# A hybrid attention block in two layers on one core: the MLP's and the latents' norms by fp32r products with ones, one inverse for both latents, two turned products and a joined maximum moved

## The reference

```python
for l in range(DEPTH):
    xn = rms_norm(x, attn_norm[l])
    (nsa_q, kv_c, kv_s, kv_w, nsa_g, cq, ckv, k_rope_raw, gate_a, gate_b) = split_cols(xn @ w_in[l])
    o_a = nsa_attention(nsa_q, kv_c, kv_s, kv_w, nsa_g, cmp_pe[l], cmp_w1[l], cmp_w2[l], pos)
    o_b = mla_attention(cq, ckv, k_rope_raw, mla_q_norm[l], mla_kv_norm[l], mla_w_uq[l], mla_w_ukv[l], pos)
    x = x + (sigmoid(gate_a) * (o_a @ nsa_w_o[l]) + sigmoid(gate_b) * (o_b @ mla_w_o[l])) @ w_out[l]
    hn = rms_norm(x, mlp_norm[l])
    x = x + square(relu(hn @ w_up[l])) @ w_down[l]
return rms_norm(x, final_norm)

# in mla_attention: cq (256 wide) and ckv (128 wide) are the latents
q  = rms_norm(cq,  q_norm)  @ w_uq
kv = rms_norm(ckv, kv_norm) @ w_ukv
# rms_norm(x, g) = x * rsqrt(mean(x * x) + 1e-6) * g, over the last axis
```

## Time and profile before

| what | value |
|---|---|
| median of three runs | 1512.05 us (1511.93 to 1512.61) |
| the profiled execution | 1511.41 us |
| its span, first to last instruction | 1509.6 us |
| PE busy | 1487.3 us, 99% |
| DVE / ACT / POOL busy | 889.5 / 719.0 / 437.2 us |
| chain that ended last | PE 85%, ACT 5%, DVE 4%, issue 4% |

### The profile page before, as it was taken

How to read it: one execution, slowest core, us unless ns; L and a number is a source line. 1 busy time by engine, 2 the same in 40 slices (tenths; PEclk the granted TensorE clock), 3 DMA queues, 4 the chain that set the end, 5 groups by cost and what they waited for, 6 DMA issues and landing times.

```text
span 1509.6 us, 21031 instructions
## 1 busy us (share of the span) xinstructions
PE 1487.3 (99%) x7284; PEld 1245.0 (82%) x7284; DVE 889.5 (59%) x1543; ACT 719.0 (48%) x1312; POOL 437.2 (29%) x459
## 2 busy tenths in 40 slices
PE   8999999999999999999999999999999999999998
PEld 6888788887888888888888888888888888888886
DVE  6876766767553544535558776667575535354453
ACT  6864777873431222222367557888543222122222
POOL 1402677873020101101022046778711101010111
PEclk9999999999999999999999999999999999999999
DMA  6333121135323333333323521212432333332233
GB/s 212 125 129 134 67 85 64 57 99 181 92 90 98 98 97 97 97 97 98 98 85 125 175 84 64 78 50 82 133 121 85 97 98 98 97 97 97 97 97 112
DMA packets 43363, 154.29 MB, mean 102 GB/s; under 512 B 5441, under 2 KB 5441, under 8 KB 43281
## 3 DMA queue, kind: packets, MB, share of 16 engines
q1 hardware_dynamic: 37296, 133.77, 28.0%
q0 software_dynamic: 5696, 18.94, 3.5%
q10 hardware_dynamic: 288, 0.52, 0.1%
HBM read 142.73 MB, written 10.49 MB: 101 GB/s over the span
## 4 chain that ended last, share of the span: by engine, by line
PE 85%; ACT 5%; DVE 4%; issue 4%; DMA 1%; POOL 0%; POOLq 0%; DVEq 0%; SPq 0%; ACTq 0%
PE G L1530 14%; PE G L1531 13%; PE G L1532 13%; PE O L1532 9%; PE O L1531 9%; PE O L1530 9%; PE O L1822 3%; PE T L1799 3%; PE T L1530 2%; PE T L1532 2%; PE T L1531 2%; PE S L1774 2%; PE O L1605 1%; ACT wsplit L645 1%; PE S L1780 1%
## 5 line engine op out<-in xcount | busy, mean ns | idle before, releaser
L645 ACT ACTIVATE wsplit<-stage 128x1024 fp32r<-128x1024 f32 x227 | 240.1, 1058 | 593.1 <-PE G L1532 270.5
L1019 DVE TENSOR_TENSOR wsplit<-stage,wsplit 128x1024 fp32r<-128x1024 f32 x180 | 259.7, 1443 | 78.3 <-ACT wsplit L645 78.1
L631 POOL TENSOR_TENSOR F<-Y 128x512 f32<-128x512 f32 x64 | 68.4, 1069 | 637.3 <-DVE Y L1488 637.3
L1530 PE MATMUL G<-xg,wsplit 128*128 128x512 f32 x560 | 223.1, 398 | 7.9 <-DVE wsplit L1045 6.9
L1531 PE MATMUL G<-xg,wsplit 128*128 128x512 f32 x560 | 219.5, 392 | 0.0
L1532 PE MATMUL G<-xg,wsplit 128*128 128x512 f32 x560 | 219.4, 392 | 0.0
L529 POOL TENSOR_TENSOR wsplit<-stage,wsplit 128x1024 fp32r<-128x1024 f32 x46 | 111.2, 2418 | 124.8 <-ACT wsplit L645 124.3
L1258 DVE CUSTOM_DVE_ANT_0 F<-S,F 128x512 f32<-128x512 f32 (+3 forms) x176 | 89.1, 506 | 88.8 <-PE S L1774 60.9
L818 ACT ACTIVATE F<-F,nmx 128x512 f32<-128x512 f32 (+3 forms) x176 | 101.4, 576 | 65.2 <-DVE nmx L1258 62.8
L1530 PEld LDWEIGHTS G<-xg,wsplit 128*128 128x128 f32 x560 | 105.6, 189 | 29.7 <-DVE wsplit L1045 6.9
L1530 PE MATMUL G<-area,wsplit 128*128 128x512 f32 x320 | 124.7, 390 | 0.3
(11 more groups left out here) (300 smaller groups left out, 3042.0 us busy)
## 6 DMA issues: line engine op xcount, KB each, us to landing
stage<-units SPq DMA_DIRECT2D x229, 512.0 KB, 3.5
stage_n<-units_n SPq DMA_DIRECT2D x20, 512.0 KB, 3.7
gates<-Y POOLq DMA_DIRECT2D x32, 256.0 KB, 2.9
E<-gates POOLq DMA_DIRECT2D x24, 256.0 KB, 3.0
F<-gates POOLq DMA_DIRECT2D x8, 256.0 KB, 3.9
x<-x_in SPq DMA_DIRECT2D x3, 512.0 KB, 6.5
rope<-tables POOLq DMA_DIRECT2D x1, 768.0 KB, 6.7
out<-F SPq DMA_DIRECT2D x3, 256.0 KB, 2.3
```

The lines of the kernel that those rows point to most:

```text
L631: pool.tensor_tensor(F[:, m % 2, :], Y[:, m % 2, :], Y[:, m % 2, :], ALU.mult)\
L645: act.activation(wslot(u)[:, 0, :], staged(u), ACT.Copy).then_inc(s_whin if u in SN else s_whi, 1)
L1019: dve.tensor_tensor(wslot(u)[:, 1, :], staged(u), wslot(u)[:, 0, :], ALU.subtract)\
L1530: pe.matmul(dst, a(0), b(0), start=first, stop=False)
```

## The change

For the latents, ACT rounds the two sums of squares (`c_squares_hi`), POOL takes their rests, and behind `MISC` four fp32r products with a matrix of halves, zeros and ones leave the mean of `ckv`'s squares on half of the partitions and that of `cq`'s on the other half, in one bank. ACT takes one root of 128x512 (`c_root`), DVE inverts 128x512 at once (`c_inverse`, behind `W1 5`, that is behind the second gate), ACT copies the halves to the partitions that lack them (`c_factors`, behind `W2K`), and the three scalings (`c_norm`) go behind `W1 6`, behind `W1 7` and into step 1. For the MLP, ACT rounds the sum of squares, DVE takes the rest, PE adds over the partitions by two fp32r products in the second tile (`wide_sum`), ACT takes a root and DVE an inverse of 128x512; the split of `up`'s fourth unit goes ahead of the first square. `WT 0` and `WT 1` are in steps 10 and 12. The joined maximum stands behind `probs_lo`.

```diff
-FILL[11].append((("WT", 0), 0))
-FILL[13].append((("WT", 1), 0))
+FILL[10].append((("WT", 0), 0))
+FILL[12].append((("WT", 1), 0))
...
+            for n, value in enumerate((0.5, 0.0, 1.0)):
+                pool.memset(halves[:, 64 * n:64 * n + 64].bitcast(F32), value).then_inc(s_halves, 1)
...
+                pool.wait_ge(s_csqhi, l + 1)
+                pool.tensor_tensor(CSQ[:, 0:4:2, :], csq[:, 0:3:2, :], CSQ[:, 1:4:2, :], ALU.subtract).then_inc(s_csqlo, 1)
...
+            def squares_hi(l):
+                act.wait_ge(s_sqadd, l * (2 * KT) + 2 * KT)
+                act.activation(SQ[:, 0, :], F[:, 2, :], ACT.Copy).then_inc(s_sqhi, 1)
+            def wide_root(l):
+                act.wait_ge(s_sqall, l + 1)
+                act.activation(rs[:, :], SB[0][:, :], ACT.Sqrt, scale=1.0 / D, bias=eps).then_inc(s_wide, 1)
...
+                def c_squares_hi():
+                    act.wait_ge(s_csq, l * 3 + 3)
+                    act.wait_ge(s_csum, l + 1)
+                    act.activation(CSQ[:, 1:4:2, :], csq[:, 0:3:2, :], ACT.Copy).then_inc(s_csqhi, 1)
                 def c_root():
-                    act.wait_ge(s_cms, l + 1)
-                    for kind in range(2):
-                        ins = act.activation(crc[:, 1, kind, :], g_tile(("CM", 0))[:, QT * kind:QT * kind + QT], ACT.Sqrt,
...
+                    act.wait_ge(s_cspread, l + 1)
+                    act.activation(csq[:, 0, :], g_tile(("CB", 0))[:, :], ACT.Sqrt, scale=1.0 / 128, bias=eps)\
+                        .then_inc(s_croot, 1)
+                def c_factors():
+                    act.wait_ge(s_cinv, l + 1)
+                    act.activation(csq[0:64, 2, :], csq[64:128, 0, :], ACT.Copy)
+                    act.activation(csq[64:128, 2, :], csq[64:128, 0, :], ACT.Copy).then_inc(s_cfactor, 1)
+                    act.wait_ge(s_cfactor, l * 2 + 1)
+                    act.activation(csq[64:128, 0, :], csq[0:64, 0, :], ACT.Copy).then_inc(s_cfactor, 1)
...
                     if item == ("Q", 2):
-                        c_root()
+                        c_squares_hi()
                     if name == "MISC":
                         q_hi(2)
                         swap_key()
+                        c_root()
...
+                    if item == ("W2K", 0):
+                        c_factors()
...
                         if isinstance(f, int) and m == 0:
-                            root(l * 2 + 1)
-                        split_hi(l, U_MLP + m + 2, f)
+                            squares_hi(l)
+                        if not (isinstance(f, int) and m == 1):
+                            split_hi(l, U_MLP + m + 2, f)
                         if isinstance(f, int) and m == 0:
-                            spread(l * 2 + 1)
+                            wide_root(l)
+                            split_hi(l, U_MLP + m + 3, f)
...
+            def squares_lo(l):
+                dve.wait_ge(s_sqhi, l + 1)
+                dve.tensor_tensor(SQ[:, 1, :], F[:, 2, :], SQ[:, 0, :], ALU.subtract).then_inc(s_sqlo, 1)
+            def wide_factors(l):
+                dve.wait_ge(s_wide, l + 1)
+                dve.reciprocal(rs[:, :], rs[:, :]).then_inc(s_rsmlp, 1)
...
-                def c_diagonals():
...
+                def c_inverse():
+                    dve.wait_ge(s_croot, l + 1)
+                    dve.reciprocal(csq[:, 0, :], csq[:, 0, :]).then_inc(s_cinv, 1)
                 def c_norm(c):
-                    dve.wait_ge(s_cspread, l * 2 + (c // 2 + 1))
+                    dve.wait_ge(s_cfactor, l * 2 + 2)
                     gain = par[:, PR_QN + c:PR_QN + c + 1]
-                    dve.scalar_tensor_tensor(E[:, c, :], E[:, c, :], gain, g_tile(("CB", c // 2))[:, :],
+                    dve.scalar_tensor_tensor(E[:, c, :], E[:, c, :], gain, csq[:, c // 2 * 2, :],
...
                     if item == ("Q", 2):
-                        c_diagonals()
+                        dve.sem_inc(s_gfree, 1)
                     if name == "MISC":
                         q_lo(2)
                         key_sum()
-                        for c in range(3):
-                            c_norm(c)
+                        dve.wait_ge(s_croot, l + 1)
+                        dve.sem_inc(s_gfree, 2)
...
+                    if item == ("W1", 5):
+                        c_inverse()
+                    if item == ("W1", 6):
+                        c_norm(0)
+                    if item == ("W1", 7):
+                        c_norm(1)
...
                         max_of(i)
-                        if joins(i) is not None:
-                            max_of(joins(i))
...
                     if 0 <= i - LAG_SPLIT < NJ:
                         probs_lo(i - LAG_SPLIT)
+                    if joins(i) is not None:
+                        max_of(joins(i))
...
+                    if i == 1:
+                        c_norm(2)
...
                         if isinstance(f, int) and m == 0:
-                            norm_diagonals(l * 2 + 1)
+                            squares_lo(l)
                             split_lo(l, U_MLP + m + 2, f)
-                            dve.wait_ge(s_rs, l * 2 + 2)
+                            wide_factors(l)
+                            dve.wait_ge(s_rsmlp, l + 1)
...
-                def c_mean_squares():
...
-                def c_spread(kind):
...
+                def c_spread():
+                    free(("CB", 0))
+                    pe.wait_ge(s_halves, 3)
+                    pe.wait_ge(s_csqlo, l + 1)
+                    for kind in range(2):
+                        for c in range(2):
+                            ins = pe.matmul(g_tile(("CB", 0))[:, :], halves[:, 64 * kind:64 * kind + P], CSQ[:, 2 * kind + 1 - c, :],
+                                            start=kind == 0 and c == 0, stop=kind == 1 and c == 1)
+                    ins.then_inc(s_cspread, 1)
...
+                def wide_sum():
+                    pe.wait_ge(s_sqlo, l + 1)
+                    for c in range(2):
+                        ins = pe.matmul(SB[0][:, :], ones_r[:, :], SQ[:, c, :], start=c == 0, stop=c == 1)
+                    ins.then_inc(s_sqall, 1)
...
-                            before = lambda k: spread(l * 2 + 1) if k == 5 else None
+                            before = lambda k: wide_sum() if k == 4 else None
                         tile(last_tile(m)[:, :], u, xg, before)
-                        if isinstance(f, int) and m == 0:
-                            mean_square(l * 2 + 1)
```

More of the change, by code:

```diff
@@ L261, in build @@
         constb = sb("constb", [P, 3, P], BF16)
-        ones = sb("ones", [P, P], F32)
+        ones_r = sb("ones", [P, P], R32)
+        halves = sb("halves", [P, 192], R32)
         par_all = sb("par_all", [P, L * NPAR + KT], F32)
@@ L294, in build @@
         cosR, sinR = Y[:, 0, :], Y[:, 1, :]
+        ones = ones_r[:, :].bitcast(F32)
+        SQ = area[:, 8192:9216].rearrange("p (c n) -> p c n", c=2)
         G = [bank("G0"), bank("G1")]
@@ L413, in build @@
         s_tab = sem("s_tab")
+        s_sqhi, s_sqlo, s_sqall, s_wide, s_rsmlp = sems("s_sqhi", "s_sqlo", "s_sqall", "s_wide", "s_rsmlp")
+        s_halves = sem("s_halves")
+        s_csqhi, s_csqlo, s_croot, s_cinv, s_cfactor = sems("s_csqhi", "s_csqlo", "s_croot", "s_cinv", "s_cfactor")
         s_xhi, s_xlo = sems("s_xhi", "s_xlo")
@@ L866, in _ @@
                     act.wait_ge(s_par, l + 1)
-                    root(l * 2)
+                    root(l)
                     split_hi(l, BIG[3])
@@ L1006, in _ @@
                     split_hi(l, NU + 1)
-            root(L * 2)
-            act.wait_ge(s_rec, L * 2 + 1)
+            root(L)
+            act.wait_ge(s_rec, L + 1)
             for b in range(0, KT, 2):
@@ L1146, in nsa_gates @@
                     dve.tensor_scalar(gt[:, :, :], gt[:, :, :], 0.5, 0.5, ALU.mult, ALU.add).then_inc(s_gfree, 1)
-                def c_diagonals():
-                    dve.wait_ge(s_crms, l + 1)
-                    chain.mark(dve.reciprocal(crc[:, 0, :, :], crc[:, 1, :, :]))
-                    chain.wait()
-                    dve.sem_inc(s_gfree, 1)
-                    for kind in range(2):
-                        ins = dve.tensor_tensor(csq[:, kind, :].rearrange("p (q n) -> p q n", q=QT),
-                                                ident.unsqueeze(1).broadcast_to([P, QT, P]),
-                                                crc[:, 0, kind, :].unsqueeze(2).broadcast_to([P, QT, P]), ALU.mult)
-                    ins.then_inc(s_cdiag, 1)
+                def c_inverse():
+                    dve.wait_ge(s_croot, l + 1)
+                    dve.reciprocal(csq[:, 0, :], csq[:, 0, :]).then_inc(s_cinv, 1)
                 def c_norm(c):
-                    dve.wait_ge(s_cspread, l * 2 + (c // 2 + 1))
+                    dve.wait_ge(s_cfactor, l * 2 + 2)
                     gain = par[:, PR_QN + c:PR_QN + c + 1]
```

(37 more changed lines are left out.)

31 lines of the change are left out of this document (13 added, 18 removed).

## The result

The changed kernel takes 1517.85 us (median of seven executions, 1514.08 to 1518.45) against 1511.93 for the kernel before on the same chip: a ratio of 1.0033, with a 95% interval of 1.0024 to 1.0043. It is slower by a third of a per cent, 7.2 us above the forecast of 1510.6 and outside its range. The profiled execution is the shortest of the seven: 1514.08, with a span of 1512.2. Its mean granted clock is .997; that of the other six is .996 to .993, and that of the kernel before .998 to 1.000.

A forecast was written before the change was run, and what follows sets the result against it. PE, busy for 99% of the span, was taken as the bound. Per layer -2.69 + 0.62 + 3.45 - 0.70 - 1.38 = -0.70, two layers -1.4: from 1512.05 to 1510.6 us, range 1506.8 to 1515.2.

The forecast's parts named there:

- the third rival: PE's clock falls in the new wait at the compressed scores, 1.9 us a fall; one fall 0.17, two 0.13.
- that idle stretch: Program's end: PE's clock falls near 1506.1, after 2.9 us idle; the new wait being at least as long decides.
- two falls: PE's clock falls behind the new wait in both layers: 1514.4, or 1516.8 with a long inverse, middle 1515.6; chance 0.13.
- The prediction's other place, the start: Program start, after 6.91 us of idling: PE at 1.2 GHz, nine products taking 3.6 + 0.4 us instead of 9 x 0.23.
- Latents' products, -2.69: Around Q 2 and MISC: plain fp32 products of 3.60 us become four fp32r products of 0.91, 2.69 us a layer less.
- The wait at the gates' transposes, +0.62: PE's gates' transposes, now earlier, wait for key_products on DVE: 0.62 us a layer comes back, bounds 0 and 1.2.
- The inverse and its wait, +3.45: Inverse of 3.58 us on DVE ahead of kc_lo: PE waits 3.45 us a layer more at the first compressed scores.
- The estimate of 4.27 us: Length of the 128x512 inverse on DVE by the Trainium skill's repeat count of 8; would end the sum at 1512.0.
- Turns and joined maximum, -0.70: Steps 10 and 15, 0.5 for turns and 0.2 for the maximum: 0.7 us a layer less, bounds 0 and 1.9.
- The MLP's norm, -1.38: MLP's first two tiles: norm costing 1.84 us becomes two fp32r products of 0.46, 1.38 us a layer less, chain hidden.
- the short inverse: Rival: inverse on DVE takes 0.69 us, new wait 0.6, time 1504.9; chance 0.06.

The follow-up runs named there:

- a wait of 1.95: Changed kernel with kc_hi behind the first of ACT's three copies, so PE waits 1.95 us in layer 0: 1511.50 us (1509.33 to 1512.53).
- the run that kept PE busy: Changed kernel plus 14 products whose sum nothing reads, ahead of the whole GATE 3 tile and so of PE's wait for kc_lo: 1511.02 us.
- the first experiment: Changed kernel with the latents' inverse behind kc_lo on DVE and its copies behind GATE 3's splits on ACT: 1505.34 us, ratio 0.9953; its theory said 1503.7.
- the latents' part alone: Kernel before with only the latents' part of the change, its inverse behind kc_lo on DVE: 1507.93 us against 1511.88.
- the wait alone: Kernel before plus an inverse ahead of kc_lo on DVE and three copies ahead of kc_hi on ACT, which nothing reads: 1523.08 us.
- the turns and the joined maximum alone: Kernel before with only the turns at steps 10 and 12 and the late joined maximum: 1510.70 us against 1511.88, ratio 0.9993.
- the first try at filling: Changed kernel plus 14 unread products in the compressed scores' first piece, which queued behind the wait for kc_lo: 1526.42 us.
- the wait of 2.74: Changed kernel with kc_hi behind the second of ACT's three copies, so PE waits 2.74 us in layer 0: 1514.75 us (1510.39 to 1517.03).

## Why the prediction was wrong

**The step that failed** is the judgement on the third rival, the fall of PE's clock. The prediction worked it out with its place (behind the new wait), its sign and its condition ("if the new wait is at least like that idle stretch", 2.9 us), and gave it 0.13 for two falls, because "one case at the end is no rule for every such wait". By its own numbers the condition was met: the forecast wait was 3.45. So the forecast wait and the two falls should not have been given separate chances: the wait came out as forecast, and the falls came with it in both layers of the trace. The mean clock of each of the seven runs (.993 to .997) says the same. Filling the same wait with work took 6.8 us off the time, and that is what the step was worth.

**Two things of the rival's price were off.** Even held for certain, two falls gave 1514.4, which is 3.4 under the median. A fall was put at 1.9 us; the profiled execution shows 1.7 a layer, close to it. But the median lies 3.8 above the profiled execution, at a mean clock of .995 where that has .997. The traces of two other kernels show falls of 6.8 us in place of 3.4 behind such a wait, 1.7 us more each, and four show a fall near the program's end, 1.7 each. Two of these would make up most of the difference; where the clock was low in the longer runs of the changed kernel itself no trace shows. And the condition of 2.9 us was read from one place where the clock fell in an idle engine; inside the program a wait of 1.95 was enough. The prediction's other place, the start, is weaker than it says: the first products there are 0.45 apart, near the pace of half clock, but in the kernel before the profile's clock column reads 1.00 there:

```profile
7.00:8.00 1.00, 1.00 (x3) 0.81 (x4) 1.00 (x2) 0.37 (x2) 0.00 (x0) 1.00 1.07 426
```

The Trainium skill ("TensorE: Matmul & The Clock Gate", Part 1) says that an idle PE goes to half clock and recovers by sustained work. The traces agree: half clock at the end of the waits of 1.95 to 3.39 or up to 1.6 us behind it, and full clock again 3.4 or 6.8 us later with PE working nearly all along.

**The terms of the sum, a layer.**

- *Latents' products, -2.69.* Right. The four fp32r products take 0.98, where 0.91 was forecast:

```profile
86.40 1.07 PE L1712 MATMUL G<-pcT,halves 128*128 128x512 f32 x4
87.38 1.22 PE L1647 MATMUL O<-narrow,area_b 128*128 128x256 f32 x8
88.75 0.40 PE L1635 MATMUL T<-constf,E 24*128 24x24 f32 x4 [0.15 <-issue]
```

- *The wait at the gates' transposes, +0.62.* Right in kind. From the W1 unit to the transposes it is 88.75 - 87.38 = 1.37, of which the unit is 0.95: 0.42. The two terms together were -2.07. From the end of `Q 2`'s tile to the W1 unit behind `Q 3`'s tile it now takes 94.65 - 79.98 = 14.67, where it took 97.17 - 80.09 = 17.08: 2.41 less. The rows before and after:

```profile
97.17 1.19 PE L1605 MATMUL O<-narrow,area_b 128*128 128x256 f32 x8
```

```profile
79.98 1.11 PE L1647 MATMUL O<-narrow,area_b 128*128 128x256 f32 x8
...
94.65 1.11 PE L1647 MATMUL O<-narrow,area_b 128*128 128x256 f32 x8
```

- *The inverse and its wait, +3.45.* Right: 3.35 for the inverse, where the earlier trace rows gave 3.58, and 3.39 for the wait. The estimate of 4.27 us that the prediction worked out from the Trainium skill ("VectorE: DVE Perf Modes", section "First, the fixed hardware budget") is 0.9 too long; the measurement, 3.35, decides for the rows.
- *Turns and joined maximum, -0.70.* Too large. The traces show 0.25 a layer (38.72 in place of 38.97 in the changed kernel) and 0.32 (38.65, alone); the median of the run alone, 0.6, is too noisy to speak against them. Nearly all of the 1.23 came back, not 0.7 of it. In the changed kernel the queue on DVE ahead of step 15's transposes is just the one that the prediction listed:

```profile
171.46 1.40 DVE L1281 TENSOR_TENSOR pcT<-O,pcT 64x512 fp32r<-64x512 f32 x2
172.89 0.69 DVE L1201 TENSOR_TENSOR cn<-E,cn 128x512 fp32r<-128x512 f32 x1
173.61 0.42 DVE L1289 CUSTOM_DVE_ANT_0 F<-S,F 128x256 f32<-128x256 f32 x1
...
174.04 0.53 DVE L1299 TENSOR_TENSOR area_b<-T,area_b 128x384 fp32r<-128x384 f32 x1
```

- *The MLP's norm, -1.38.* Right: the two tiles and the norm take 417.85 - 406.52 = 11.33, where they took 12.74, 1.41 less. DVE's chain ends in time:

```profile
416.05 3.35 DVE L1090 RECIPROCAL rs<-rs 128x512 f32<-128x512 f32 x1 [1.52 <-ACT rs L684]
419.44 0.69 DVE L1528 SCALAR_TENSOR_TENSOR Y<-G,rs 128x512 f32<-128x512 f32 x1
420.05 1.21 DVE L1052 TENSOR_TENSOR wsplit<-stage,wsplit 128x1024 fp32r<-128x1024 f32 x1
```

The split ends at 421.3, and PE takes that unit up at 423.29: 2.0 of cover, where 1.7 was forecast.

The sum without the clock came out at 1511.02 in the run that kept PE busy, 0.4 from the forecast. Part of that is luck: the turns brought 0.4 a layer less than forecast and the latents' part 0.3 more. The durations were right all the same, within 0.25 us each, and the time was wrong because a rival followed from one of the forecast's own terms. (One recorded sum is off by rounding: the short inverse gives 1510.6 - 2 x 2.9 = 1504.8. Nothing hangs on it.)

**Still open.** Where the changed kernel loses more than 3.4 us to the clock in its longer runs. And the 1.5 us by which the first experiment stays above 1503.7 and the sum of its parts: the fall near the end accounts for some of it in some runs. The wait of 1.02 for GpSimd's split belongs to what the forecast left out, but the latents' part alone has it too, so it does not tell the first experiment from that sum.

## What to carry to other kernels

Price a new wait of the matrix engine twice: by its length, and by what the clock loses behind it; for the waits of 1.95 to 3.39 the second was 0.7 to 1.0 of the first here. Before such a wait is accepted, look for a pause of the waiting chain's engine a little later (here 3.24 us between two sums of compressed scores, 12 us after the place where the inverse stood) and put the long operation there, or else give the matrix engine work ahead of the wait. And when an operation is moved forward on a busy engine, move what stands around it back by the same length, or the wait may only change its place, as it did here.

## What was not expected of the hardware

The clock falls around the moment when PE takes up its work again, and mostly behind it. Of the ten falls at such a wait nine came 0 to 1.6 us after PE's first product and one 0.1 before it (the wait alone, layer 1: a clock of 0.53 in the us from 870, PE's first product at 870.19). The distance does not go with the length of the wait: behind 3.39 and 3.38 in the changed kernel it is 1.6 in layer 0 and 0.4 in layer 1. So a trace that is read only up to the end of a wait may show nothing of it.

The stretches at half clock had two lengths: 3.4 us in twelve of the fourteen that lie ahead of a program's last product, 6.8 in two. Those two are the ones that began earliest, with PE's first product (2.74, layer 0) and 0.1 before it.

A fall can come without any long wait. In the run with the inverse put behind, the clock is at half from 1494.4 to 1497.8, behind the last norm's one-column products, while PE turns the result in products of 128x128 and is 100% busy:

```profile
1493.00:1494.00 1.00, 0.84 (x8) 0.62 (x6) 0.00 (x0) 0.33 (x1) 0.45 (x1) 1.00 0.00 0
1494.00:1495.00 1.00, 1.00 (x8) 1.00 (x9) 0.18 (x1) 0.28 (x2) 0.00 (x0) 0.70 0.00 0
...
1497.00:1498.00 1.00, 1.00 (x8) 1.00 (x7) 0.75 (x1) 0.00 (x0) 0.06 (x1) 0.59 0.65 248
```

Three other traces have one there too: the turns and the joined maximum alone (1501.2 to 1504.6), the first try at filling (1515.2 to 1518.6) and the wait of 2.74 (1504.6 to 1508.0). The other ten traces, that of the kernel before among them, have none. All kernels make the same products there, so the change does not bring it by itself; what does was not studied.
